# Loading, splitting and using the first four weight blocks of a transformer kernel in halves

## The reference

```python
h = rms_norm(x, g[0])        # x * rsqrt(mean(x*x) + EPS) * gain
proj = h @ w_in              # 1024 rows of w_in: 8 k steps of 128
...
ang = positions[..., None] * inv_freq
cos, sin = jnp.cos(ang), jnp.sin(ang)     # rope, used after the latents' norms
```

## Time and profile before

| | |
|---|---|
| device time, median of 3 runs | 1768.34 us (1767.92 to 1768.91) |
| span of the profiled execution | 1764.2 us |
| PE busy in it | 1737.4 us, 98% |
| PEld / DVE / ACT / POOL busy | 1445.3 / 785.8 / 662.9 / 876.9 us |
| chain that ended last | PE 90%, DVE 5%, ACT 2% |
| DMA, mean over the span | 90 GB/s |
| DMA in its first fortieth (44 us) | 190 GB/s |

### The profile page before, as it was taken

How to read it: one execution, slowest core, us unless ns; L and a number is a source line. 1 busy time by engine, 2 the same in 40 slices (tenths; PEclk the granted TensorE clock), 3 DMA queues, 4 the chain that set the end, 5 groups by cost and what they waited for, 6 DMA issues and landing times.

```text
span 1764.2 us, 22985 instructions
## 1 busy us (share of the span) xinstructions
PE 1737.4 (98%) x8243; PEld 1445.3 (82%) x8243; DVE 785.8 (45%) x1225; ACT 662.9 (38%) x1039; POOL 876.9 (50%) x473
## 2 busy tenths in 40 slices
PE   8999999999999999999999999999999999999999
PEld 6887888888888877878888888889878888888887
DVE  6558654301331479956430133137856344444200
ACT  6338543312322456554321232135357332222221
POOL 3457545444444469755544444445445544444442
PEclk9999999999999999999999999999999999999999
DMA  5531123223333213123333332322210233332332
GB/s 190 133 98 59 37 72 107 95 95 96 96 96 99 80 48 108 60 84 95 103 99 96 96 95 95 95 84 72 87 49 14 95 95 96 97 101 98 96 107 71
DMA packets 46073, 158.45 MB, mean 90 GB/s; under 512 B 5744, under 2 KB 6000, under 8 KB 46000
## 3 DMA queue, kind: packets, MB, share of 16 engines
q1 hardware_dynamic: 46000, 157.45, 28.5%
HBM read 153.10 MB, written 2.10 MB: 88 GB/s over the span
## 4 chain that ended last, share of the span: by engine, by line
PE 90%; DVE 5%; ACT 2%; issue 1%; POOL 1%; DMA 0%; SPq 0%; DVEq 0%; POOLq 0%; ACTq 0%
PE PS L1834 26%; PE PS L1835 26%; PE PS L1836 26%; PE PS L1903 2%; DVE PS L1219 1%; PE PS L1939 1%; PE PS L1934 1%; PE PS L1935 1%; PE PS L2095 1%; PE PS L1844 1%; PE PS L1876 0%; PE PS L1976 0%; DVE PS L1211 0%; PE PS L2118 0%; PE PS L2119 0%
## 5 line engine op out<-in xcount | busy, mean ns | idle before, releaser
L548 POOL TENSOR_TENSOR wl<-raw,wh 128x1024 fp32r<-128x1024 f32 x216 | 523.0, 2422 | 623.2 <-ACT wh L742 198.3
L1835 PE MATMUL PS<-XLR,wh 128*128 128x512 f32 x1216 | 474.2, 390 | 0.0
L1834 PE MATMUL PS<-XHR,wh 128*128 128x512 f32 x888 | 348.8, 393 | 6.3 <-POOL wl L618 5.8
L1836 PE MATMUL PS<-XHR,wl 128*128 128x512 f32 x888 | 346.4, 390 | 0.0
L1834 PE MATMUL PS<-HH,wh 128*128 128x512 f32 x688 | 267.6, 389 | 0.0
L1835 PE MATMUL PS<-HL,wh 128*128 128x512 f32 x688 | 267.6, 389 | 0.0
L1836 PE MATMUL PS<-HH,wl 128*128 128x512 f32 x688 | 267.6, 389 | 0.0
L1835 PEld LDWEIGHTS PS<-XLR,wh 128*128 128x128 f32 x1216 | 229.1, 188 | 47.0
L728 ACT ACTIVATE wh<-raw 128x1024 fp32r<-128x1024 f32 x123 | 128.9, 1056 | 242.2 <-PE PS L1836 197.6
L1834 PEld LDWEIGHTS PS<-XHR,wh 128*128 128x128 f32 x888 | 167.4, 188 | 42.0 <-POOL wl L618 6.2
L1836 PEld LDWEIGHTS PS<-XHR,wl 128*128 128x128 f32 x888 | 167.4, 188 | 35.4
(11 more groups left out here) (344 smaller groups left out, 2561.6 us busy)
## 6 DMA issues: line engine op xcount, KB each, us to landing
raw<-weights SPq DMA_DIRECT2D x287, 512.0 KB, 3.5
X<-x_t SPq DMA_DIRECT2D x8, 256.0 KB, 6.7
out_t<-X SPq DMA_DIRECT2D x8, 256.0 KB, 4.7
KH<-rope_h SPq DMA_DIRECT2D x4, 128.0 KB, 4.7
KL<-rope_l SPq DMA_DIRECT2D x4, 128.0 KB, 5.5
QH<-XHR SPq DMA_DIRECT2D x16, 32.0 KB, 2.0
QL<-XLR SPq DMA_DIRECT2D x16, 32.0 KB, 2.0
pos_i<-positions SPq DMA_DIRECT2D x1, 256.0 KB, 8.5
```

The lines of the kernel that those rows point to most:

```text
L548: pool.tensor_tensor(wl[:, j], raw[:, j], wh[:, j].bitcast(F32), ALU.subtract).then_inc(w_lo, 1)
L1834: pe.matmul(out, wa, xa, start=start, stop=False)
L1835: pe.matmul(out, wa, xb, start=False, stop=False)
L1836: return pe.matmul(out, wb, xa, start=False, stop=stop)
```

## The change

Blocks 0 to 3 are loaded in two halves of four k steps (128x512, 256 KB each) with a semaphore of their own for the first halves (`raw_first`, `first_hi`, `first_lo`). The first half of block 0 and 1 comes behind slice 0 and 1, those of blocks 2 and 3 behind slice 3; the second halves of blocks 0 to 3 come behind slices 4 to 7. ACT and DVE split the halves in the same turns. PE's order is rewritten with `both` alone. The work between the last split and PE's `spread("x0")` is unchanged on all engines, and so is everything after it.

```diff
+HALF_SLOTS = SLOTS // 2
+FIRST_HALVES = {0: (0,), 1: (1,), 3: (2, 3)}
+SECOND_HALVES = {4: (0,), 5: (1,), 6: (2,), 7: (3,)}
...
             for k in range(KT):
                 sp.dma_start(X[:, k], x_t[:, k]).then_inc(x_in[k], 16)
-                if k % 2 == 0:
-                    sp.dma_start(raw[:, k // 2], weights[k // 2]).then_inc(raw_in[k // 2], 16)
+                for j in FIRST_HALVES.get(k, ()):
+                    sp.dma_start(raw[:, j, 0:HALF_SLOTS], weights[j, :, 0:HALF_SLOTS]).then_inc(raw_first[j], 16)
+                for j in SECOND_HALVES.get(k, ()):
+                    sp.dma_start(raw[:, j, HALF_SLOTS:], weights[j, :, HALF_SLOTS:]).then_inc(raw_in[j], 16)
...
-                if k % 2 == 0:
-                    hi(k // 2)
+                for j in FIRST_HALVES.get(k, ()):
+                    sc.wait_ge(raw_first[j], 16)
+                    sc.activation(wh[:, j, 0:HALF_SLOTS], raw[:, j, 0:HALF_SLOTS], ACT.Copy).then_inc(first_hi, 1)
+                for j in SECOND_HALVES.get(k, ()):
+                    sc.wait_ge(raw_in[j], 16)
+                    sc.activation(wh[:, j, HALF_SLOTS:], raw[:, j, HALF_SLOTS:], ACT.Copy).then_inc(w_hi, 1)
...
-                if k % 2 == 0:
-                    v.wait_ge(w_hi, k // 2 + 1)
-                    tt(wl[:, k // 2], raw[:, k // 2], f(wh[:, k // 2]), ALU.subtract).then_inc(w_lo, 1)
+                for j in FIRST_HALVES.get(k, ()):
+                    v.wait_ge(first_hi, j + 1)
+                    tt(wl[:, j, 0:HALF_SLOTS], raw[:, j, 0:HALF_SLOTS], f(wh[:, j, 0:HALF_SLOTS]),
+                       ALU.subtract).then_inc(first_lo, 1)
+                for j in SECOND_HALVES.get(k, ()):
+                    v.wait_ge(w_hi, j + 1)
+                    tt(wl[:, j, HALF_SLOTS:], raw[:, j, HALF_SLOTS:], f(wh[:, j, HALF_SLOTS:]),
+                       ALU.subtract).then_inc(w_lo, 1)
...
             def both(t, k):
-                high(t, k, k + 1)
-                return low(t, k, k + 1)
+
+                pe.wait_ge(first_hi if k < HALF_SLOTS else w_hi, t + 1)
+                pe.wait_ge(xh, k + 1)
+                pe.wait_ge(xl, k + 1)
+                pe.matmul(PS[:, t], wh[:, t, k], XH[:, k], start=k == 0, stop=False)
+                pe.matmul(PS[:, t], wh[:, t, k], XL[:, k], start=False, stop=False)
+                pe.wait_ge(first_lo if k < HALF_SLOTS else w_lo, t + 1)
+                return pe.matmul(PS[:, t], wl[:, t, k], XH[:, k], start=False, stop=k == KT - 1)
...
+            for t, k in ((0, 0), (0, 1), (1, 0), (1, 1), (0, 2), (1, 2), (0, 3), (1, 3)):
+                both(t, k)
+            for t in (2, 3):
+                for k in range(HALF_SLOTS):
+                    both(t, k)
+            for t, k in ((0, 4), (0, 5), (1, 4), (1, 5), (0, 6), (1, 6), (2, 4), (2, 5), (2, 6)):
+                both(t, k)
             for t in range(3):
                 both(t, 7).then_inc(blocks_done, 1)
-            low(3, 0, 6)
-            both(3, 6)
+            for k in range(HALF_SLOTS, KT - 1):
+                both(3, k)
             stat("x0")
             both(3, 7).then_inc(blocks_done, 1)
```

More of the change, by code:

```diff
@@ L290, in build @@
         consts_r = sem("consts_r")
+        raw_first = [sem(f"raw_first{j}") for j in range(RING)]
+        first_hi, first_lo = sem("first_hi"), sem("first_lo")
         w_hi = sem("w_hi")
@@ L1968, in norm_out @@
                 keep_busy(W_UPDATE, PS[:, T % 4])
[L1970 to L1984, removed]
-            def both(t, k):
-                high(t, k, k + 1)
-                return low(t, k, k + 1)
+            def both(t, k):
+                pe.wait_ge(first_hi if k < HALF_SLOTS else w_hi, t + 1)
[5 more added lines that the diff above has]
+                return pe.matmul(PS[:, t], wl[:, t, k], XH[:, k], start=False, stop=k == KT - 1)
             pe.wait_ge(consts, NCONST)
```

## The result

| | median | lowest to highest | runs |
|---|---|---|---|
| before | 1767.92 us | 1766.55 to 1768.91 | 5 |
| changed | 1775.59 us | 1774.53 to 1775.95 | 5 |

The changed kernel takes 1.0042 of the time of the kernel before, 95% interval 1.0031 to 1.0054: 7.7 us slower. The profiled execution of the changed kernel has a span of 1773.8 us, 9.6 us above the 1764.2 of the one before. Why the spans differ by more than the medians is told further down.

What follows compares the result with a forecast made beforehand. PE, busy 98% of the span, was taken as the bound. +7.0 us for the late factor and +2.3 for the clock gave +9.3, on the median 1768.3 + 9.3 = 1777.6 us; range 1769.0 to 1781.0.

Steps and rivals of the forecast that it cites:

- The mechanism: Opening: PE's lead starts POOL early, POOL and DVE take turns, rcol comes at 43.0 us, PE waits, clock halves.
- 7.0 for the factor: PE's wait for rcol: PE passes the x0 factor at 43.2 us instead of 36.20, 7.0 us later.
- 2.3 for the clock: Behind PE's wait for the factor: matmuls at the half clock add 2.3 us.
- Who met whom: DVE's angles beside POOL: operation 8 free, 9 to 14 each behind a POOL instruction, 15.6 us, to 42.5.
- Part one: PE's opening: slice 2's matmul stays at 9.96 us, the 78th starts at 24.8 instead of 28.2, 3.4 us earlier.
- Part two: ACT, DVE and SP in the opening: data sets the pace, DVE's first sum near 17.3 us, 0.4 us earlier.
- The cover that I gave the extra instructions: Opening: DVE's four more subtractions and SP's four more transfers cost nothing extra, hidden under the wait for data.
- the case: Whole kernel: the early opening makes the factor late, +9.3 us, from +6 to +12; chance 0.65.
- the upper end of the clock's term: Behind PE's wait for the factor: the whole 6.8 us stretch at half pace, given as 3.2 us.
- the kept lead: Rival: three-operand DVE operations slip under memsets, rcol by 34 to 35 us, 1.5 to 2.5 us faster; chance 0.23.
- the middle: Rival: only operation 15 held up by block 5, rcol near 36.7 us, +0.7 to +3.0 us; chance 0.12.
- the change doesn't do what it says: Rival on loads: half transfers carry a fixed cost, PE's lead shrinks towards 1 us; no chance of its own.

Runs made afterwards that it cites:

- run 1: Changed kernel; POOL, behind block 4, waits for DVE's x0 factor, then blocks 5 and 6, memsets, block 7: 1764.69 us, ratio 0.9988 to the kernel before.
- run 5: Changed kernel; DVE makes the x0 factor before the second angle, POOL behind block 4 waits for both angles: 1763.84 us, ratio 0.9982 to the kernel before.
- run 6: Kernel before, without the change; x0 factor before the second angle on DVE, POOL behind block 4 waits for both angles: 1767.17 us, ratio 0.9999.
- run 3: Changed kernel with 40 thrown-away matmuls on PE right before its wait for the x0 factor: 1775.67 us, ratio 1.0040 to the kernel before.
- run 8: Changed kernel measured once more, unedited, beside the kernel before on the same chip: 1774.97 us, ratio 1.0040.
- run 7: Changed kernel with POOL's two memsets moved from behind block 4 to behind block 5: factor at 36.45 us; no kernel time given.
- run 10: Changed kernel with POOL's two memsets behind block 5, measured a second time: 1770.35 us against 1768.92 of the kernel before, one run each.
- run 4: Kernel before with whole blocks, loads and splits as before, and only PE's new order of matmuls: 1767.38 us, one run.

## Why the prediction was right

**The mechanism held.** POOL's early start, one DVE operation behind each POOL instruction, `rcol` near 43.0 (43.10), PE at 43.2 (43.33), a wait of some 10 us (9.71), half clock behind it (to 48.1). The terms: 7.0 for the factor, measured 43.33 - 36.20 = 7.1; 2.3 for the clock, measured 2.2. Their sum was 9.3 on the profiled span, and the spans differ by 9.6. At 153.84, where PE was at 144.46 before, the difference is 9.4, so nothing more of weight is added behind the opening, as foretold. In runs 1 and 5, where POOL is held back, all of the loss is gone and PE's lead comes through; run 6 shows that the same edits bring nothing without that lead.

**Who met whom was off by one.** The prediction let operation 8 run free and held up 9 to 14. In the trace POOL began 0.02 us ahead of operation 8, so 8 to 13 were held up and 14 ran free. The six turns took about 14.7 us (from 27.18 to the 43.10 of the factor less operations 14 and 15) where 15.6 were foretold; POOL's start was 0.25 later than the 26.93 taken, and one more operation, 0.7, came behind. The three nearly cancel. In run 3 the pairs were those of the prediction (operation 8 took 0.43 at 27.29, block 4 began at 27.49), and its factor came at 43.23: either pairing gives the same time.

**Two terms below that were off, and their difference came right by luck.** Part one had the 78th matmul at 24.8, 3.4 us earlier; it was 25.48, 2.7 earlier. I had left slice 2 where it was, since the same bytes come before it. ACT's timeline shows it late:

```profile
8.99 0.72 ACT L810 ACTIVATE XHR<-X,vec 128x512 fp32r<-128x512 f32 x1 [1.09 <-DMA X<-x_t]
```

It was released at 8.99, and PE's matmul of slice 2 moved from 9.96 to 10.64. Which piece comes late varies from execution to execution with the same loads: here PE waits 0.76 us for slice 2; in run 8 it waits 0.25 us for slice 1, in run 3 1.20 and in run 7 1.72. No run tries what sets it.

Part two had DVE's sums 0.4 us earlier; they began at 17.99, 0.3 later than the 17.68 of the earlier trace rows. I had taken the data as ACT's pace to the end and a half block at 0.6. ACT's starts in the second part of the opening say otherwise:

```profile
13.58 0.63 ACT L816 ACTIVATE wh<-raw 128x512 fp32r<-128x512 f32 x1
14.24 0.72 ACT L810 ACTIVATE XHR<-X,vec 128x512 fp32r<-128x512 f32 x1
14.95 0.64 ACT L816 ACTIVATE wh<-raw 128x512 fp32r<-128x512 f32 x1
15.61 0.72 ACT L810 ACTIVATE XHR<-X,vec 128x512 fp32r<-128x512 f32 x1
16.28 0.63 ACT L816 ACTIVATE wh<-raw 128x512 fp32r<-128x512 f32 x1
```

No wait for a DMA stands in any of them: ACT works without a pause at 0.65 to 0.7 an instruction, and a whole block used to take it 0.97 (14.78 to 15.75), where two halves take some 1.3. The cover that I gave the extra instructions was gone, and ACT set the pace. What decides the case is the difference of the two shifts: 3.4 - 0.4 = 3.0 foretold, 2.7 + 0.3 = 3.0 measured. The case came out right by a difference of which neither part was right. On top of these, the upper end of the clock's term is a slip: half of the 6.8 us stretch is 3.4 and not 3.2; nothing hangs on it.

**The predicted time was 2.0 us too high** (1777.6 against 1775.6), and that is the last step: I added 9.3 to the median of three, 1768.34, as though the profiled execution stood 4.1 us below it by what lies around a span. In every execution of which both are given, the time lies some 1.8 us above the span (1775.59 and 1773.8). So the profiled execution of before took an estimated 1766.0, near the lowest of that kernel's runs (1765.97 to 1770.62 over the 21 of the largest comparison), and most of its distance to the median was not overhead but spread. 1766.0 + 9.6 is the 1775.6 measured. For the same reason the medians differ by only 7.7: the median of the kernel before, 1767.92, stands 1.9 us above its profiled execution, and that of the changed kernel on its own. The spread goes with the clock: of these 21 runs, those at a mean granted clock of 0.996 took 1765.97 to 1767.22 us, those at 0.995 1766.72 to 1768.91, those at 0.994 or less 1767.02 to 1770.62. The changed kernel, with its certain half clock at 43 us, has runs within 1.4 us.

**The rivals.** Neither the kept lead nor the middle came in any of the ten timed runs of the changed kernel (1774.51 to 1775.95). Runs 10 and 7 come near them in time, but with POOL's work in another order: run 10 with 4.4 us of wait, and run 7, in which PE's lead over DVE was 1.5 us (POOL's start 0.57 earlier than before, DVE's angles 0.93 later), with 0.9. As far as ten runs tell, the case was surer than the 0.65 it was given. In run 3, too, where PE waited 1.20 us in the opening, POOL started early enough for the full delay. An opening like that of run 7 in the changed kernel itself was not seen. That the change doesn't do what it says is out: PE's lead was 2.7 us, and 0.4 without the halves (run 4).

## What to carry over

An edit that makes the bounding engine earlier moves everything that it releases. Before counting the gain, list what the released engines will then run beside, and which of it can't run at once: here a POOL instruction that reads SBUF and a DVE operation with two SBUF inputs, or a tensor_scalar and a memset, run one after the other, and a small operation can wait for nearly the full length of a big one. If a short result waits at the end of a long chain on such an engine (the factor behind fifteen angle operations), move it forward, and hold the other engine back until the chain is through; the same opening that cost 7.7 us then gains 3.2.

## What the runs showed beside that

- A DVE operation on four elements a partition can wait as long as a whole tile: `floor<-sd`, 0.13 us alone, took 2.09 at 38.20 in run 10, under POOL's subtraction from 37.87; both its inputs lie in SBUF. The reciprocal next to it, with one SBUF input, took its 0.18.
- A wait of 1.3 to 1.4 us in one stage is followed by 6.8 us at half clock in two of the twelve executions (run 3 at 153.9, run 5 at 143.5) and passed at full clock by the others, so single spans differ by over 2 us with no cause in the edit.
- Splitting a 128x1024 copy on ACT in two costs 0.3 to 0.35 us a block (0.97 to some 1.3), where DMA at 0.66 us for 256 KB leaves no room for it.
